# First channel group of a causal depthwise convolution: 36 banded phase products in place of 24 diagonal products and seven taps on other engines

## The reference, cut to what matters

```
h = a * sigmoid(gate)                                  # 1024 tokens x 256 channels
h = conv_general_dilated(h, conv_w, window_strides=(1,), padding=[(CONV_WIDTH - 1, 0)],
                         feature_group_count=D_C) + conv_b      # depthwise, 31 taps, causal
h = layer_norm(h, ln_g, ln_b);  y_c = silu(h)
```

## Time and profile before

| | |
|---|---|
| three executions | 990.85, 991.65, 996.98 us (median 991.65) |
| profiled execution | span 989.0 us; its own device time is not listed |
| PE busy | 906.2 us, 92% |
| DVE busy | 687.2 us, 69% |
| ACT busy | 560.2 us, 57% |
| POOL busy | 360.3 us, 36% |
| the chain that ended last | PE 45%, DMA 9%, DVE 6%, ACT 2%, issue 2% |

### The profile page before, as it was taken

How to read it: one execution, slowest core, us unless ns; L and a number is a source line. 1 busy time by engine, 2 the same in 40 slices (tenths; PEclk the granted TensorE clock), 3 DMA queues, 4 the chain that set the end, 5 groups by cost and what they waited for, 6 DMA issues and landing times.

```text
span 989.0 us, 15968 instructions
## 1 busy us (share of the span) xinstructions
PE 906.2 (92%) x4804; PEld 712.6 (72%) x4805; DVE 687.2 (69%) x1033; ACT 560.2 (57%) x805; POOL 360.3 (36%) x271
## 2 busy tenths in 40 slices
PE   6999999999898899999918999999999999999990
PEld 6877888744466567888807888888878888888770
DVE  5339888898789875737687747889888854234276
ACT  5256567686787665702233647777777743225342
POOL 0000079999999980000001112222332321111137
PEclk9999999999999999999959999999999999999995
DMA  8550111000000100533576879999999987552475
GB/s 234 146 139 22 43 43 65 1 0 2 1 2 1 44 1 23 169 119 130 230 286 216 268 253 317 391 403 382 404 403 382 404 282 241 177 148 45 108 243 211
DMA packets 63486, 172.54 MB, mean 174 GB/s; under 512 B 19297, under 2 KB 33633, under 8 KB 51120
## 3 DMA queue, kind: packets, MB, share of 16 engines
q1 hardware_dynamic: 55664, 143.85, 39.4%
q0 software_dynamic: 7488, 27.07, 11.0%
q10 hardware_dynamic: 288, 1.05, 0.3%
HBM read 142.79 MB, written 26.74 MB: 171 GB/s over the span
## 4 chain that ended last, share of the span: by engine, by line
PE 45%; DMA 9%; DVE 6%; ACT 2%; issue 2%; DVEq 0%; ACTq 0%; POOLq 0%; POOL 0%; SPq 0%
PE ps L472 13%; PE ps L474 12%; PE ps L473 12%; DMA raw<-in_w_gate 9%; PE ps L950 2%; DVE wlo L1762 1%; PE ps L824 1%; ACT whi L1248 1%; DVE sm L1608 1%; PE ps L791 1%; PE ps L986 1%; PE ps L874 1%; PE ps L811 1%; DVE xgT_lo L1772 0%; DMA xg<-x_d,slot_token 0%
## 5 line engine op out<-in xcount | busy, mean ns | idle before, releaser
L1762 DVE TENSOR_TENSOR wlo<-raw,whi 128x2048 fp32r<-128x2048 f32 x96 | 216.1, 2288 | 51.9 <-ACT whi L1248 51.8
L1248 ACT CAST whi<-raw 128x2048 fp32r<-128x2048 f32 x96 | 180.3, 1911 | 50.0 <-DMA raw<-in_w_gate 17.5
L472 PE MATMUL ps<-whi,xgT_hi 128*128 128x512 f32 x384 | 152.0, 396 | 6.7 <-DVE xgT_lo L1772 6.7
L474 PE MATMUL ps<-whi,xgT_lo 128*128 128x512 f32 x384 | 149.8, 390 | 0.0
L473 PE MATMUL ps<-wlo,xgT_hi 128*128 128x512 f32 x384 | 149.6, 390 | 0.0
L472 PEld LDWEIGHTS ps<-whi,xgT_hi 128*128 128x128 f32 x384 | 72.3, 188 | 22.9 <-issue 7.1
L472 PE MATMUL ps<-xT_hi,w_hi 128*128 128x512 f32 (+1 forms) x224 | 87.0, 388 | 1.7 <-DVE xT_lo L1360 1.7
L1986 POOL COPY idx_now<-slot_token 128x1 int32 (+1 forms) x24 | 8.0, 334 | 218.2 <-PE ps L950 218.2
L473 PE MATMUL ps<-xT_lo,w_hi 128*128 128x512 f32 (+1 forms) x224 | 85.7, 383 | 0.0
L474 PE MATMUL ps<-xT_hi,w_lo 128*128 128x512 f32 (+1 forms) x224 | 85.7, 383 | 0.0
L474 PEld LDWEIGHTS ps<-whi,xgT_lo 128*128 128x128 f32 x384 | 72.1, 188 | 15.4
(11 more groups left out here) (333 smaller groups left out, 1923.9 us busy)
## 6 DMA issues: line engine op xcount, KB each, us to landing
raw<-in_w_gate SPq DMA_DIRECT2D x32, 1024.0 KB
raw<-in_w_up SPq DMA_DIRECT2D x32, 1024.0 KB
raw<-in_w_down SPq DMA_DIRECT2D x32, 1024.0 KB
w_raw<-in_w_in SPq DMA_DIRECT2D x14, 512.0 KB, 4.0
x_tok<-in_x SPq DMA_DIRECT2D x8, 512.0 KB, 7.8
wo_raw<-in_w_o SPq DMA_DIRECT2D x16, 256.0 KB, 2.8
x_res<-in_x SPq DMA_DIRECT2D x16, 256.0 KB, 3.4
x_d<-xa SPq DMA_DIRECT2D x4, 512.0 KB, 6.0
```

The lines of the kernel that those rows point to most:

```text
L472: pe.matmul(out, l_hi, r_hi, start=start, stop=False)
L474: return pe.matmul(out, l_lo, r_hi, start=False, stop=stop)
L1248: act.copy(whi[:, n, :], raw[:, n, :]).then_inc(gu_hi if n < 4 else dn_hi, 1)
L1762: dve.tensor_tensor(wlo[:, n, :], raw[:, n, :], f32(whi[:, n, :]), ALU.subtract).then_inc(gu_lo if n < 4 else dn_lo, 1)
```

## The change

Tokens are dealt into four time phases (token t has phase t mod 4), and the 128 channels into four quarters of 32. DVE writes the gated input by phase into `phased` (the same memory as `hpad[:, 0]`, four stretches of 264 elements, the first 8 of each zero). SP copies it with 16 small DMAs into `stack_h`, where for quarter g the partitions are (phase, channel) and the free axis is time divided by four. For each quarter nine products of 256 columns are accumulated: their stationary operand is a 128x128 matrix whose rows are (input phase, channel) and whose columns are (output phase, channel), non-zero where the channels agree, so that one product covers up to 16 pairs of phases. 4 x 9 = 36 products hold all 31 taps. `CONV_FROM` is `PROJECTIONS + 4`. DVE builds the matrices, one quarter an instruction of 1152 elements a partition, from weights that it has put in place with 32 small copies (`phase_taps`, two calls behind unit iq0,0 and two behind iq1,0) and a mask of four 32x32 unit matrices that POOL adds up at the start. ACT's `item` becomes `late_item` in the rounds and behind them. The products stand three at a time ahead of the last twelve units, in banks 4 and 5 by turns, quarter 2 and 3 each waiting until ACT has evicted the quarter two before. ACT evicts a quarter with four instructions (one an output phase, 32 partitions x 256 elements, writing every fourth element), three quarters among the rounds of the search and the last behind all 25 rounds. The steps `conv0` and `tap`, POOL's two taps of group 0 and its additions of `extra` are gone.

```diff
-TAPS_PE = 24
-TAPS_EARLY = 18
-TAPS_PER_ROUND = 4
+PHASES, CH = 4, P // 4
+SPAN = 9
+CONV_PER_UNIT = 3
-TAPS_DVE = 5
...
-    steps.append(("conv0",))
...
-        if p in range(len(PAIRS) - 3 - TAPS_DVE, len(PAIRS) - 3):
-            steps.append(("tap", p - (len(PAIRS) - 3 - TAPS_DVE)))
...
+                if COLS[j][0] == "q0":
+                    sp.wait_ge(pads_set, 1)
+                    sp.wait_ge(unit_dve, seen(BY_DVE, UNITS.index(("a0", 1, [c[0] for c in COLS].index("a0")))))
+                    for g in range(PHASES):
+                        for s in range(PHASES):
+                            sp.dma_start(stack_h[s * CH:(s + 1) * CH, g, :], phased[g * CH:(g + 1) * CH, s, :]
+                                         ).then_inc(phased_in, 16)
...
-            def tap(w):
+            def conv_part(n):
+                g, j = divmod(n, SPAN)
+                if n == 0:
                     pe.wait_ge(unit_act, seen(BY_ACT, PROJECTIONS - 1))
                     pe.wait_ge(unit_dve, sum(BY_DVE))
+                    pe.wait_ge(phased_in, 16 * PHASES * PHASES)
+                if j == 0:
+                    pe.wait_ge(toep_set, g + 1)
+                    if g >= 2:
+                        pe.wait_ge(conv0, PHASES * (g - 1))
+                last = pe.matmul(conv_bank(g), toep[:, g, 4 * j:4 * j + 4, :].rearrange("p q c -> p (q c)"),
+                                 stack_h[:, g, j:j + 256], start=j == 0, stop=j == SPAN - 1)
...
-                if k >= PROJECTIONS + 4:
-                    tap(taps)
+                if k >= CONV_FROM:
+                    for n in range(CONV_PER_UNIT):
+                        conv_part((k - CONV_FROM) * CONV_PER_UNIT + n)
                 unit(k, between)
-            for w in range(taps, TAPS_EARLY):
-                tap(w)
...
                     if r in (1, 2):
-                        pe.wait_ge(conv0, 1)
+                        pe.wait_ge(conv0, PHASES * PHASES)
...
+            def conv_out(g):
+                act.wait_ge(conv0_mm, g + 1)
+                for q in range(PHASES):
+                    act.activation(conv[g * CH:(g + 1) * CH, 0, PHASES - 1 - q::PHASES], conv_bank(g)[q * CH:(q + 1) * CH, :],
+                                   ACT.Identity, bias=phase_bias[q * CH:(q + 1) * CH, g:g + 1]).then_inc(conv0, 1)
+            def late_item(k, between):
+                item(k, between)
+                g, part = divmod((k - CONV_FROM + 1) * CONV_PER_UNIT - CONV_PER_UNIT, SPAN)
+                if k > CONV_FROM and part == 0:
+                    conv_out(g - 1)
...
+            conv_out(PHASES - 1)
...
+                    if ti == 0:
+                        v0 = 8 + t0 // PHASES
+                        dve.tensor_tensor(phased[:, :, v0:v0 + P].rearrange("p r x -> p x r"),
+                                          src.rearrange("p (x r) -> p x r", r=PHASES),
+                                          sig[:, 0, t0:t0 + n].rearrange("p (x r) -> p x r", r=PHASES), ALU.mult
+                                          ).then_inc(unit_dve, 1)
...
+            def phase_taps(s):
+                rows = slice(s * CH, (s + 1) * CH)
+                for g in range(PHASES):
+                    dve.tensor_copy(toep_w[rows, g, 5 - s:5 - s + TAPS], convw[g * CH:(g + 1) * CH, 0:TAPS]).then_inc(toep_in, 1)
+                    dve.tensor_copy(phase_bias[rows, g:g + 1], convb[g * CH:(g + 1) * CH, 0:1]).then_inc(toep_in, 1)
...
-                elif taps < TAPS_PE:
-                    dve.tensor_tensor(diag[:, taps:taps + n, :], unit_diag.unsqueeze(1).to_broadcast([P, n, P]),
...
+                elif toeps < PHASES:
+                    wide = [P, 4 * SPAN, CH]
+                    dve.tensor_tensor(toep[:, toeps], unit_mask.unsqueeze(1).to_broadcast(wide),
+                                      toep_w[:, toeps].unsqueeze(2).to_broadcast(wide), ALU.mult).then_inc(toep_set, 1)
...
-            pool.wait_ge(conv0, 1)
...
-            pool.wait_ge(extra_set, TAPS_DVE)
...
```

More of the change, by code:

```diff
@@ L425, in program @@
         tri_set, pads_set, searched = sem("tri_set"), sem("pads_set"), sem("searched")
[L426 to L427 removed]
+        toep_set, conv0_mm, conv0, conv1, pooled, pool_chain = (
+            sem(n) for n in ("toep_set", "conv0_mm", "conv0", "conv1", "pooled", "pool_chain"))
+        toep_in, phased_in = sem("toep_in"), sem("phased_in")
         tap_mul, both_in, both_mm = sem("tap_mul"), sem("both_in"), sem("both_mm")
@@ L736, in _ @@
             pe.wait_ge(dve_set, 1)
-            def tap(w):
-                if w == 0:
+            def conv_part(n):
+                g, j = divmod(n, SPAN)
+                if n == 0:
                     pe.wait_ge(unit_act, seen(BY_ACT, PROJECTIONS - 1))
                     pe.wait_ge(unit_dve, sum(BY_DVE))
[L742 to L747, removed]
+                    pe.wait_ge(phased_in, 16 * PHASES * PHASES)
[5 more added lines that the diff above has]
+                                 stack_h[:, g, j:j + 256], start=j == 0, stop=j == SPAN - 1)
+                if j == SPAN - 1:
                     last.then_inc(conv0_mm, 1)
-            taps = 0
             for k, between in PLAN[1:]:
-                if k >= PROJECTIONS + 4:
-                    tap(taps)
-                    taps += 1
+                if k >= CONV_FROM:
+                    for n in range(CONV_PER_UNIT):
+                        conv_part((k - CONV_FROM) * CONV_PER_UNIT + n)
                 unit(k, between)
-            for w in range(taps, TAPS_EARLY):
-                tap(w)
             def projected(hf, t, i):
@@ L802, in _ @@
                         projected(0, t, i)
-                elif kind == "conv0":
-                    for w in range(TAPS_EARLY, TAPS_PE):
-                        tap(w)
                 elif kind == "pt":
@@ L1145, in _ @@
                     if step[1] == 0:
-                        act.wait_ge(conv1, 2 * (2 * TAPS - TAPS_PE - TAPS_DVE + 1))
+                        act.wait_ge(conv1, 2 * TAPS)
                         act.wait_ge(ring_act, seen(RING_ACT, RING_OF["pw", 1, 1]))
                     mix_split(step[1])
-                elif kind == "conv0":
-                    act.wait_ge(conv0_mm, 1)
-                    act.activation(conv[:, 0, :], pair(2), ACT.Identity, bias=convb[:, 0:1]).then_inc(conv0, 1)
                 elif kind == "exp":
@@ L1421, in item @@
                 unit(k)
+            def phase_taps(s):
[3 more added lines that the diff above has]
+                    dve.tensor_copy(phase_bias[rows, g:g + 1], convb[g * CH:(g + 1) * CH, 0:1]).then_inc(toep_in, 1)
+            dve.wait_ge(toep_in, 1)
+            phases = list(range(PHASES))
             for p in PLAN[:LAST_IDX + 1]:
                 item(*p)
+                if UNITS[p[0]][:2] in (("iq0", 0), ("iq1", 0)):
+                    for _ in range(2):
+                        phase_taps(phases.pop(0))
             rest = [p for p in PLAN[LAST_IDX + 1:] if p[0] < PROJECTIONS]
@@ L1438, in _ @@
             dve.wait_ge(masked_s, len(BLOCKS))
-            taps = 0
+            dve.wait_ge(toep_in, 1 + 2 * PHASES * PHASES)
+            toeps = 0
             for r in range(ROUNDS):
@@ L1470, in _ @@
             link(dve.tensor_tensor(lo, low, top_score, ALU.mult))
-            assert not rest and taps == TAPS_PE
+            assert not rest and toeps == PHASES
             def choose(b, k):
@@ L1858, in _ @@
             pool.affine_select(ident[:], ident[:], [[-1, P]], ALU.not_equal, 1.0, 0, 1).then_inc(ident_set, 1)
+            pool.wait_ge(ident_set, 2)
+            for n in range(1, PHASES):
+                pool.tensor_tensor(phase_mask[:], ident[:, 0:CH] if n == 1 else phase_mask[:], ident[:, n * CH:(n + 1) * CH],
+                                   ALU.add).then_inc(ident_set, 1)
+                pool.wait_ge(ident_set, 2 + n)
             pool.wait_ge(stack_in[0], 16 * 20)
```

72 lines of the change are left out of this document (29 added, 43 removed).

## The result

| | before | after |
|---|---|---|
| median of the runs | 992.76 us (5 runs, 990.85 to 996.98) | 1002.08 us (5 runs, 999.36 to 1007.02) |
| span of the profiled execution | 989.0 us | 1000.3 us |
| PE busy | 906.2 us | 891.2 us |
| mean granted clock | 0.970 | 0.948 |

The change is slower: ratio 1.0088, 95% interval 1.006 to 1.0117, some 9 us, where I forecast 990.2 us. The profiled executions differ by 11.3 us. PE lost only 15 us of its busy time where I expected 26. Between the first key unit and the second attention scores it lost 19.3 us (59.7 to 40.4), at a granted clock of 0.75 where before had 1.00; another 3.4 us came back behind the second scores, and 0.9 ahead of the first unit.

What follows compares the result with a forecast made beforehand. PE's projections were taken to set the time to about 193.8 us, then DVE's search, then an attention chain of DVE, PE and ACT. -0.7 behind the search and -0.8 late in the attention gave -1.5 on 991.65: 990.2 us, range 986 to 995.

Steps and rivals of the forecast that it cites:

- PE's products: PE's convolution: 41.3 us removed, 72 records at 0.215 us (15.5 us) added; worth no time by itself, the search covers it.
- Builds: DVE in the search: five exposed builds (2.45 us) become three of 1.21 us (3.63), +1.2 us.
- The evictions: ACT in the rounds: 0.30 us an instruction, 1.2 a quarter; quarter 0 covered, quarters 1 and 2 cost 0.8 and 1.1.
- My rival's 0.70: ACT's strided evictions at 0.70 us each: search ends 6.1 us later, second scores 4.9 later, 995.7 us in all; chance 0.17.
- The rest of the search's sum: DVE's search: builds +1.2, vanished wait -1.3, evictions +1.9, together +1.7 us, ends +1.3 and +6.1.
- slack of a round with a build: ACT in a search round with a build: quarter 0's evictions fit, 4.9 of 5.0 us, and cost nothing.
- 0.3 of late start: ACT's count in a round may start some 0.3 us late before DVE notices; subtracted from quarter 1's cost.
- vanished wait -1.3: DVE's search: the 1.33 us wait while the last value unit held ACT goes, since PE is earlier.
- Behind the search: From the search's end to the second scores: 250.5 us against 251.16, -0.7, ends -1.7 and +4.9.
- Late in the attention: DVE's tap at 339.21 us, ahead of a row maximum for which ACT idles: -0.8 us, between -0.8 and -7.75.
- the 2 us that I set as a sign of error: A change above 2 us from the second scores to the end would mean the attention's bound was misread.
- Edits at nothing: DVE's small copies, SP's 16 DMAs, the gated input by phase and the masks: under idle time or without effect, 0 us.

Runs made afterwards that it cites:

- the kernel without the taps: The kernel before without taps 24 to 30 of the first channel group (seven multiply-adds on DVE and POOL), diagonal products and search untouched: 1009.88 us.
- 20 products before the search's end: The changed kernel with 20 products of 512 columns that nobody reads, behind the last unit: 1002.54 us, ratio 1.0109.
- The kernel with four evictions: The changed kernel with four 128-partition evictions for sixteen, products over three banks, POOL moving the sixteen pieces: 991.14 us, ratio 0.9972.
- its two variants: The kernel with four evictions, once with 24 unread products behind the last unit (990.61 us), once with the last eviction moved into a round (991.03 us).
- the kernel with adjacent writes: The changed kernel with its sixteen evictions writing 256 adjacent elements into a separate area, read in token order: 998.61 us, ratio 1.0061.

## Why the prediction was wrong, point by point

- **PE's products:** right. 0.215 us a record was taken, 0.215 measured (2.15 us for three and a unit). PE's busy time fell by 15 us, not 26; its clock fell to 0.75 from the first unit to the second scores, which I had at half only around 246 to 249.
- **Builds:** 1.21 us predicted for what a build adds to a round, 1.14 measured (DVE's rounds with one take 4.97 to 4.99 us, plain ones 3.84; the instruction itself takes 1.35). Three such rounds of some 5.0 us, as said.
- **The evictions, the step that failed.** The term was "I take 0.30 an instruction, 1.2 us a quarter"; it measured 0.73 and 2.95. Two errors of like size: of the missing 0.43, the stride is 0.20 (0.25, for the 0.05 that I allowed), and some 0.23 is the plain price: a copy of 256 takes 0.38 in a row of its like, not the 0.25 that I read off between a copy and an exponential, and the bias adds 0.11. The strided weight load was the wrong neighbour: a read, on another engine. My rival's 0.70 was an upper bound that I called unlikely; the real price lies past it, and no row had given that bound either. By the starts of DVE's counts the three rounds take 5.18, 6.92 and 6.81 us, so the term was worth 1.3, 3.1 and 3.0 us for quarters 0, 1 and 2, where I had 0, 0.8 and 1.1: 7.4 us instead of 1.9.
- **The rest of the search's sum:** right. With the measured 2.95 us a quarter in its own terms (slack of a round with a build, 0.3 of late start, builds +1.2, vanished wait -1.3) it gives 1.62 + 2.53 + 2.83 - 0.1 = 6.9 us, and 7.16 was measured; with 1.93 it gives 3.8, and 4.09 was measured. At 0.70 an instruction the same terms give 6.4, not the 6.1 that I wrote. But the point from which the rival decides, 0.42 us an instruction, was too high: at 0.48 us the kernel lost not some 1 us but 6.
- **Behind the search:** predicted -0.7 at the second scores, and +4.9 in the rival. Measured +7.2: what the search lost went through in full, and the 2.4 us that I had as a gain here did not come. Of these, 1.7 are again the evictions (the last quarter takes 2.90 us, not 1.2, and stands ahead of PE's pooling products), and 0.7 the clock (from the quarter's end to the second scores 4.97 us, where I had 4.3).
- **Late in the attention:** -0.8 predicted; -0.6 to -1.0 shown by the kernel without the taps.
- **What I did not price:** the distance from the second scores to the end grew by 3.1 us, beyond the 2 us that I set as a sign of error; with the -0.8 that I had there it is the second largest miss, 3.9 us. Its cause stays open. The stretch of half clock at 265.9 to 272.8 does not explain it, since it was weaker in the second profile (0.79) and the distance was the same; with 20 products before the search's end the stretch moved and the distance was 739.3. The kernel with four evictions, whose PE idles as long, has 735.2, but in the fastest of its twelve executions (985.64 us, 5.5 below their median), so its usual distance is nearer to 740 (an estimate); its two variants have 740.8 and 739.9. So all profiles of kernels with the new products and the full result, but for that one, lie 1.7 to 3.7 us above the 737.6 of before.
- **The account:** the profiled spans differ by 11.3 us where the sum had -1.5, a miss of 12.8. Of it, rounded, 5.5 us are the evictions in the rounds, 2.4 what stands behind the search, 3.9 the distance to the end, and 1.1 the chance at 61 to 64 us.
- **Edits at nothing:** the gated input, the copies and the DMAs cost nothing that is seen. The first key unit starts at 190.4 or 191.5 in the kernel before, by the clock at 61 to 64 us, and at 190.4 to 191.7 and once 193.4 in kernels that have all of the change up to there.

The Trainium skill's rule on SBUF ("SBUF — State Buffer", Specifications (TRN2): 16-byte lines, at least two hits in a line) had the direction: this case's traces agree, with 256 writes costing 0.04 us more at two to a line and 0.25 more at one to a line. It was worth 3.1 of the search's 7.2 us, not all of them, as the kernel with adjacent writes shows.

## What to carry to other kernels

Where an engine has slack only by the round, count its new instructions, not their elements: an instruction on 32 partitions costs as much as one on 128, so a result that falls apart into quarters should leave PSUM whole and be dealt out later by an engine that has time. Price a new instruction by a run of its own kind (same function, same operands, same step), not by one neighbour's pitch, and if the sum's sign hangs on that price, the rival at its upper bound deserves more than a sixth of the chance. And work taken off PE while another engine sets the pace buys about as much as PE was behind that engine: of 26 us of PE's work, 2.5 us came back at the second scores in the kernel with four evictions, and 1.5 in its time. Last, a stretch of half clock beside a loss is not yet its cause: look for a second profile in which the one is gone and the other is not.

## What the runs showed of the hardware that I had not expected

- ACT, 256 float32 from PSUM to SBUF: 0.38 us as a copy, 0.11 more with a per-partition bias, 0.25 more with a 16-byte step of the write, 0.04 with 8 bytes; with a bias the same on 32 and 128 partitions (adjacent and 16 bytes), and the parts add up.
- DVE's instructions on six elements take 0.17 us. Those whose inputs are both in SBUF (`sm<-sm`) took 1.18 and 1.19 us beside an addition of two tensors on POOL: two stand behind the end of the search, and in the changed kernel with the last eviction moved POOL's two additions from 256.04 (2.48 us together) run beside them. Each of the two ends within 0.1 us of one of these additions, so they look held until it is over. In the kernel with adjacent writes it was 0.58 and 1.19. Those with an operand in PSUM (`sm<-sm,ps`) kept 0.16 to 0.17 us beside such an addition (251.92 to 252.49, POOL's from 250.51 to 253.00), and the two themselves took 0.17 each in the changed kernel beside POOL's multiplication by a weight (252.32, POOL's from 251.08 to 254.19). It held DVE up by 1.4 to 2.0 us, by where POOL's taps happened to be:

```profile
255.95 0.16 DVE L1511 SCALAR_TENSOR_TENSOR sm<-sm,ps 128x6 f32<-128x6 f32 x1
256.15 1.18 DVE L1513 SCALAR_TENSOR_TENSOR sm<-sm 128x6 f32<-128x6 f32 x1
257.36 1.19 DVE L1514 TENSOR_TENSOR sm<-sm 128x6 f32<-128x6 f32 x1
```

- Stretches of half clock come and go between profiles of one kernel, 1.1 us at 61 to 64 us, 2.1 us in the first expert's products: two profiles of one kernel can differ by that much ahead of any change. Over all profiles the first key unit starts between 190.4 and 193.4 us, though nothing ahead of it differs but the change's own copies.
